# The sum of squares of the recurrence's outputs: from one float32 product to two rounded ones

## The reference, cut to what matters

```python
def hgrn2_mixer(h, lower_bound, w_in, gnorm_w, w_out):
    proj = h @ w_in
    q, f, i, z = jnp.split(proj, ...)
    ...
    o = chunked_gated_recurrence(q, k, v, log_f)
    o = o * lax.rsqrt(jnp.mean(o * o, axis=-1, keepdims=True) + NORM_EPS) * gnorm_w
    o = o.reshape(B, T, REC_WIDTH) * jax.nn.silu(z)
    return o @ w_out
```

## Time and profile before

| | |
|---|---|
| median of three runs | 3657.53 us |
| the profiled execution | 3661.34 us, span 3660.0 us |
| TensorE, matmuls | 3461.1 us busy (95%) |
| TensorE, weight loads | 2777.6 us (76%) |
| VectorE | 2063.2 us (56%) |
| ScalarE | 1719.2 us (47%) |
| GpSimd | 1353.8 us (37%) |
| mean granted clock of TensorE | 0.982 |
| the recurrence | from about 930 to 1950 us of the span |
| norm products (L1457) in it | 32, of 2 matmul records each, 32.9 us busy |

### The profile page before, as it was taken

The page is one execution under the profiler, slowest core; times in us unless marked ns, Lnnn a source line. Parts: engine busy times, 40 slices in busy tenths (PEclk is TensorE's granted clock), DMA queues, the critical chain, the costliest instruction groups (busy, mean ns, idle before and its releaser), DMA issues. The chain is left out here.

```text
span 3660.0 us, 89296 instructions
## 1 busy us (share of the span) xinstructions
PE 3461.1 (95%) x37856; PEld 2777.6 (76%) x37856; DVE 2063.2 (56%) x4664; ACT 1719.2 (47%) x3161; POOL 1353.8 (37%) x1681
## 2 busy tenths in 40 slices
PE   8999998899899999999998989999999997999999
PEld 7888785688677777777776867777777775788777
DVE  4566766755555657555555445666666665343422
ACT  3455555522555556555554344444444442444422
POOL 5433321232455554555543333232322320444332
PEclk9999999999999999999998999999999998999999
DMA  4322211222110111111012341111111113322322
GB/s 136 90 67 81 61 53 33 84 98 94 34 44 25 42 30 36 36 30 42 24 42 87 133 142 43 42 43 43 43 43 38 42 37 112 86 70 70 104 81 92
DMA packets 252267, 231.66 MB, mean 63 GB/s; under 512 B 9120, under 2 KB 223072, under 8 KB 251872
## 3 DMA queue, kind: packets, MB, share of 16 engines
q1 hardware_dynamic: 251872, 225.94, 20.2%
HBM read 192.35 MB, written 33.55 MB: 62 GB/s over the span
## 5 line engine op out<-in xcount | busy, mean ns | idle before, releaser
L196 PE MATMUL bank<-hT_cut,arena_cut 128*128 128x512 f32 x2048 | 804.2, 393 | 0.0
L189 ACT ACTIVATE arena<-bank 128x512 f32<-128x512 f32 (+1 forms) x584 | 315.5, 569 | 560.3 <-PE bank L197 272.2
L195 PE MATMUL bank<-hT_cut,arena_cut 128*128 128x512 f32 x1240 | 552.1, 445 | 0.0
L197 PE MATMUL bank<-hT_cut,arena_cut 128*128 128x512 f32 x1240 | 488.2, 394 | 0.0
L195 PE MATMUL bank<-arena_cut,hT_cut 128*128 128x512 f32 (+1 forms) x1280 | 457.9, 358 | 30.3 <-DVE arena_cut L1153 25.7
L189 ACT ACTIVATE arena<-arena 128x512 f32<-128x512 f32 (+3 forms) x674 | 349.9, 554 | 261.7 <-POOL arena L1598 199.4
L196 PE MATMUL bank<-arena_cut,hT_cut 128*128 128x512 f32 (+1 forms) x1280 | 448.1, 350 | 0.0
L196 PEld LDWEIGHTS bank<-hT_cut,arena_cut 128*128 128x128 f32 x2048 | 387.4, 189 | 79.1 <-issue 18.6
L190 ACT ACTIVATE arena<-arena 128x256 f32<-128x256 f32 (+2 forms) x336 | 210.4, 627 | 412.5 <-DVE arena L179 187.9
L2848 POOL TENSOR_TENSOR arena_cut<-arena,arena_cut 128x256 fp32r<-128x256 f32 x272 | 218.0, 831 | 411.0 <-ACT arena_cut L189 411.0
L716 POOL TENSOR_TENSOR arena_cut<-arena,arena_cut 128x256 fp32r<-128x256 f32 x288 | 215.9, 777 | 414.2 <-ACT arena_cut L189 414.1
(11 more groups left out here) (267 smaller groups left out, 7129.7 us busy)
## 6 DMA issues: line engine op xcount, KB each, us to landing
arena<-in_w_in SPq DMA_DIRECT2D x100, 512.0 KB, 3.9
arena<-in_attn_w_in SPq DMA_DIRECT2D x144, 256.0 KB, 2.8
arena<-in_rec_w_in SPq DMA_DIRECT2D x62, 512.0 KB, 4.1
x_after<-arena SPq DMA_DIRECT2D x32, 512.0 KB, 2.6
arena<-x_after SPq DMA_DIRECT2D x32, 512.0 KB, 4.0
arena<-in_x SPq DMA_DIRECT2D x16, 512.0 KB, 3.6
h_after<-hT SPq DMA_DIRECT2D x4, 2048.0 KB, 7.8
hT<-h_after SPq DMA_DIRECT2D x4, 2048.0 KB, 16.5
```

The lines of the kernel that those rows point to most:

```text
L189: return e.activation(out, a, f, bias=bias, scale=scale)
L195: pe.matmul(out, a[0], b[0], start=start, stop=False)
L196: pe.matmul(out, a[0], b[1], start=False, stop=False)
L197: return pe.matmul(out, a[1], b[0], start=False, stop=stop)
```

## The change

Before, TensorE multiplies the squares (float32) by the 128 x 128 float32 table of ones. After, ScalarE rounds the squares with a Copy into a block under its rounded name (float32r), VectorE subtracts this from the squares, in place, as the rest, and TensorE makes two rounded products in one accumulation, ones with the rounded part and ones with the rest. The ones are a rounded column of width 1, read with a stride of zero as 128 x 128. ScalarE makes that column once, ahead of the two Exp of the setup.

Where Square was followed by two yields on ScalarE, the rounding follows it at once and then three yields. TensorE's norm has three yields ahead of it and one behind, instead of two and two. VectorE's rest stands five yields behind the states, with two more before "on", where there were seven. TensorE now waits for VectorE's "lo" where it waited for ScalarE's "sq". The final yield of ScalarE's back goes; Ln and Exp stand behind its last one. The rings d_at and e_at get second names for rounded data; no block is added to them.

```diff
-    d_at, e_at = k.rooms(3, G), k.rooms(3, G)
+    d_two, e_two = [k.room_cut(G) for _ in range(3)], [k.room_cut(G) for _ in range(3)]
+    d_at, d_cut, e_at, e_cut = ([x[i] for x in two] for two in (d_two, e_two) for i in range(2))
+    ones_1 = k.room_cut(2)[1]
+    ones_cut = ones_1[:, 0:1].broadcast_to([P, P])
...
+    sq_hi, sq_lo = lambda u: d_cut[(8 * u + 7) % 3], lambda u: e_cut[(7 * u + 6) % 3]
...
             ins.then_inc(*Bpe.did("o"))
-            yield
-            yield
+            for _ in range(3):
+                yield
             b, before = kb.take("norm", u)
-            pe.wait_ge(*Ba.by("sq", u))
+            pe.wait_ge(*Bv.by("lo", u))
+            if u == 0:
+                pe.wait_ge(*set_a.by("ones"))
             if before is not None:
                 pe.wait_ge(*taken_back(*before))
-            pe.matmul(b, k.c("ones"), e_of(u, 6), start=True, stop=True).then_inc(*Bpe.did("norm"))
-            yield
+            pe.matmul(b, ones_cut, sq_hi(u), start=True, stop=False)
+            pe.matmul(b, ones_cut, sq_lo(u), start=False, stop=True).then_inc(*Bpe.did("norm"))
             yield
...
             act(a, e_of(u, 6), kb.at("o", u), ACT.Square).then_inc(*Ba.did("sq"))
-            yield
-            yield
+            a.wait_ge(*Ba.by("sq", u))
+            act(a, sq_hi(u), e_of(u, 6), ACT.Copy).then_inc(*Ba.did("hi"))
+            for _ in range(3):
+                yield
             a.wait_ge(*Bpe.by("norm", u))
             k.ln(d_of(u, 7), kb.at("norm", u), bias=k.eps_col(4 * EPS), scale=1.0 / P).then_inc(*Ba.did("ln"))
             a.wait_ge(*Ba.by("ln", u))
             act(a, d_of(u, 7), d_of(u, 7), ACT.Exp, scale=-0.5).then_inc(*Ba.did("rs"))
-            yield
...
+        act(a, ones_1, k.c("ones")[:, 0:2], ACT.Copy).then_inc(*set_a.did("ones"))
         a.wait_ge(*set_v.by("x0"))
...
-            for _ in range(7):
+            for _ in range(5):
+                yield
+            v.wait_ge(*Ba.by("hi", u))
+            v.tensor_tensor(sq_lo(u), e_of(u, 6), sq_hi(u), ALU.subtract).then_inc(*Bv.did("lo"))
+            for _ in range(2):
                 yield
             v.wait_ge(*Ba.by("rs", u))
             v.tensor_tensor(e_of(u, 6), kb.at("o", u), d_of(u, 7), ALU.mult).then_inc(*Bv.did("on"))
```

More of the change, by code:

```diff
@@ L1284, in recurrence @@
     set_v = k.steps("bounds_prepared", "sel", "lb0", "lb1", "gn", "half", "max", "x0", "x1", "sum", "rc", "share", "bb", "nb", "least", "ab")
-    set_a = k.steps("bounds_exp", "l0", "l1")
+    set_a = k.steps("bounds_exp", "ones", "l0", "l1")
     Fpe = head.products
@@ L1292, in recurrence @@
     Bpe = k.steps("back_products", "diag", "vt", *(f"l{l}" for l in range(LEVELS)), "kt", "ds", "o", "norm")
-    Ba = k.steps("back_scalar", "dx1", "dx2", "vt", *(f"dx{l}" for l in range(3, 7)), "eb", "dk", "sq", "ln", "rs")
+    Ba = k.steps("back_scalar", "dx1", "dx2", "vt", *(f"dx{l}" for l in range(3, 7)), "eb", "dk", "sq", "hi", "ln", "rs")
     Bv = k.steps("back_vector", "e1_1", "e2_1", "diag", *(x for l in range(5) for x in (f"e1_{l + 2}", f"e2_{l + 2}", f"s{l}")),
-                 "qt", "dk", "s5", "s6", "kt", "st0", "st1", "st2", "st3", "on", "out")
+                 "qt", "dk", "s5", "s6", "kt", "st0", "st1", "st2", "st3", "lo", "on", "out")
     Bp = k.steps("back_pool", *(f"d{l}" for l in range(1, 7)), "dk")
```

## The result

The changed kernel takes 3676.24 us (median of five runs, 3671.27 to 3677.63) against 3659.43 for the kernel before (3653.46 to 3661.21): 16.8 us slower, ratio 1.0043, 95% interval 1.003 to 1.0055. The forecast was 9.6 us slower, 3667 on the 3657.53 known then (3669 on the 3659.43 measured beside the change). The time lies 0.8 us inside the upper end of the wide range (3655 to 3677) and outside the forecast's own range (3662 to 3673).

The account below looks back on a forecast made before the run. TensorE was taken to bind odd windows, a chain through the other engines even ones. Odd 3.8, even 4.0 and stage end 1.8 sum to 9.6 us on 3657.5: 3667, own range 3662 to 3673, wide range 3655 to 3677.

Parts of the forecast that it names:

- The chain's delay: From Square through the norm: table load, Ln, Exp and "on" come 0.55 us later, bounds 0.40 and 1.07.
- TensorE's saving: At the norm, two rounded products replace the float32 one: 0.40 us a unit, 12.8 us over 32, if nothing else moved.
- Odd windows: Norm to norm from an odd unit, TensorE-bound before: level 2 late by 0.25 us, 15 x 0.25 = 3.8 us.
- the cover: Time in hand at level 2 in odd windows before VectorE's later work delays TensorE: some 0.3 us.
- Even windows: Norm to norm from an even unit, chain-bound: 0.07 later rounding plus 0.20 crowding, 0.27 us each, 15 x 0.27 = 4.0 us.
- Between none and both (0.36) I take 0.20: Even windows: GpSimd's quarter and differences lengthened beside VectorE by 0.15 and 0.21 us; 0.20 us assumed.
- e2: VectorE instruction of level 1, even windows: moves 0.55 us later, falling beside GpSimd's quarter and differences.
- The third rival: VectorE's subtraction between Square and norm is held up, up to 0.53 us more: 26 us slower, 3683; chance 0.09.
- The end of the stage: Unit 31, no projections beside it: delay and new steps count in full, 1.8 us, bounds 1.4 and 2.4.
- The second rival: Whole stage: TensorE is the bound and both chains have more room; 10 us less, 3647; chance 0.09.
- the fourth: Norm products with a broadcast column run at float32 pace, twice 0.75 us: some 30 us slower, 3688; chance 0.03.
- the first, without crowding: Same chain, GpSimd not crowded, weights loaded ahead: delay 0.45, some 4 us, 3661.5, no measurable change; chance 0.36.

Follow-up runs that it names:

- two squares: Changed kernel, table load early, z-weight rounding and quarters late, rounded part from a second Square of o instead of a copy; 3612.52 us, ratio 0.9859 to 0.9892.
- early orders: ScalarE's Ln table load before the norm wait, z-weight rounding and GpSimd's quarters later; 3613.51 us on the kernel before, 3618.93 on the changed one.
- work only: Changed kernel with the kernel before's yields on TensorE and ScalarE around norm, rounding, Ln and Exp; 3680.58 us, ratio 1.0045 to 1.0075.

## Why the prediction was right, and where its sizes were off

The mechanism was right: a delay on the chain from Square to "on", with too little cover. That the time fell into the wide range owes something to its width, for two of the three terms came out nearly twice as large as forecast.

**The chain's delay** was forecast as 0.55 us and measured as 0.56 (2.80 against 2.24; "on" 5.48 against 4.92). Each part held: rounding 0.63 for 0.62, rest 0.69, TensorE late by 0.17 for 0.14, the first rounded product 0.34, the copy of v over just before the norm.

**TensorE's saving** is real, and it is lost as forecast: at the norm 0.17 for the rest and 0.11 for weights that couldn't be loaded ahead, then the wait at level 2. Where two squares take the first of these away and early orders give the chain room, the odd windows keep about 0.25 of the 0.40 us.

**Odd windows**: forecast 0.25 us each, measured 0.33 in thirteen ordinary ones. Level 2 is late by 0.29: the projection product behind it starts 10.76 us after Square (1329.71) against 10.47 in the kernel before, with Square at 1312.08:

```profile
1322.55 0.50 PE L195 MATMUL bank<-oT_cut,arena_cut 128*128 128x512 f32 x1
```

So the cover, read off a merged row as some 0.3 us, was 0.27. Where the other 0.04 arise stays open.

**Even windows**: forecast 0.27, measured about 0.47 in twelve ordinary ones. The rounding came 0.07 us later, as forecast. The step that was mis-sized is "Between none and both (0.36) I take 0.20": both GpSimd instructions are lengthened, by 0.14 and 0.18, 0.32 in sum. Level 2's differences end 9.33 us after Square's start (1285.11); in the kernel before, with Square at 1278.69, they ended after 8.94:

```profile
1286.91 0.72 POOL L1598 TENSOR_TENSOR arena<-arena 128x256 f32<-128x256 f32 x1
```

The 0.39 pass on nearly unchanged to level 2 (11.75 after Square against 11.37) and level 5 (19.27 against 18.90), here in the changed kernel:

```profile
1285.11 0.60 ACT L189 ACTIVATE arena<-bank 128x512 f32<-128x512 f32 x1 [4.37 <-PE bank L1451]
```

```profile
1296.86 0.45 PE L1412 MATMUL bank<-arena 128*32 128x16 f32 x32 [1.74 <-DVE arena L1697]
...
1304.38 0.45 PE L1412 MATMUL bank<-arena 128*32 128x32 f32 x16 [1.29 <-DVE arena L1697]
```

The other 0.08 arise between 21.0 and 22.7 us after Square, at the transposed keys; why is open. By the rule of the Trainium skill (SBUF — State Buffer, Who interferes with whom) the ports that a VectorE instruction with two inputs shares with GpSimd are an exclusive lock, so the later of the two is blocked in full. VectorE's e2, the later one beside the quarter, comes near to that: it takes 0.97 us instead of 0.43, 0.54 more, as long as a quarter of 0.76 would still have had to run. GpSimd's differences don't: they start with 0.33 us of e2 to come and take 0.18 more. The 0.4 that the prediction worked out by that rule were nearer to the measured 0.32 than the 0.20 it took.

The clock explains none of this, though it changed. In eleven of the fifteen even windows TensorE's granted clock fell behind the wait at level 2, which is now 1.74 us long in ordinary windows, to 0.5, the lower of its two levels (1.2 GHz), for a part of the window: its mean there is 0.95, and TensorE is busy 32.1 us instead of 30.8. In the kernel before all even windows show 1.00. But the four windows that kept 1.00 behind the same wait lose as much (0.45 to 0.50 us) as the ordinary ones that didn't (0.46 to 0.49): the slower products only fill the wait at level 5, which is gone there. That is a sign of its own that the chain sets these windows, and not TensorE.

Two even windows lose 0.45 more in a wait for the transposed keys; why these two is open. It isn't the clock: in work only two windows lose as much at 1.00.

**Windows with h rounded besides** were "counted as the rest". This was wrong: the three lose 1.56, 0.33 and 0.88 us, 2.0 us more than forecast in sum. The third rival, a rest that is held up on VectorE, did happen here, for one norm, where VectorE makes subtractions for h first and TensorE waits 1.23 us:

```profile
1417.13 0.50 PE L1463 MATMUL bank<-arena_cut 128*128 128x512 f32 x1 [1.23 <-DVE arena_cut L1747]
```

**The end of the stage** was forecast as 1.8 us and measured as 1.75: from Square of unit 30 to the output layer's first product 33.86 us against 32.11. TensorE's wait at the last norm grew from 0.69 to 2.07 us:

```profile
1962.78 0.50 PE L1463 MATMUL bank<-arena_cut 128*128 128x512 f32 x1 [2.07 <-DVE arena_cut L1747]
...
1968.83 0.77 PE L195 MATMUL bank<-arena_cut,hT_cut 128*128 128x512 f32 x1 [5.31 <-DVE arena_cut L1153]
```

**Sum**: even windows 7.9 us for 4.0, odd 6.8 for 3.8 (2.4 of them in two windows with h), end 1.75 for 1.8: 16.4 us. The second rival (TensorE binds) and the fourth (float32 pace) are refuted by the rows; the first, without crowding, by GpSimd's.

## What to carry to other kernels

A saving on the busiest engine can be worth nothing at a step whose result others wait for: count the time from the last input to the first reader, over all engines, and ask what that chain has in hand; here 0.3 us of cover were fewer than the 0.56 that two short added instructions and one later place cost. On such a chain look first for what needn't be in it: a table load behind a wait cost 22 us, and another tensor's work ahead in two in-order queues (ScalarE's and GpSimd's, moved together) 20 more, each larger than the 12.8 us that the products could save at most. And windows with extra work on an engine are to be priced by themselves, not with the rest.

## What the runs showed of the hardware

A column of ones read with a stride of zero serves as 128 x 128 weights at full pace: its two loads at a norm take 185 and 188 ns, as against 188 to 189 for full ones, and the product behind the first starts 0.34 us later, the next 0.23. The weight load for a product behind a semaphore isn't made ahead of it: at the norm shown in the section on the result it starts with the product (0.18 us from 1320.98, the product at 1320.99), and the first product takes 0.34 us to the next start where its neighbours take 0.23. With two squares, where TensorE loses no time to the wait, it is the same (load at 1299.84, product at 1299.85, 0.33 us).
